# A seventh gather buffer, a sum-first joint between two token tiles, and four gate units moved into the second tile's block

## The chip, the core and the metric

The kernel runs on one core of a Trainium2 chip. The metric is the device time of one execution in microseconds, taken as the median of several runs. Five engines work beside each other: TensorE (PE; PEld is its weight loading), VectorE (DVE), ScalarE (ACT), GpSimd (POOL) and SyncE (SP). Each works its own queue in order and waits on semaphores. Sixteen DMA engines carry all transfers.

## The reference

One layer of each of two blocks is computed on 256 tokens of width 1024 in float32. The parts that matter here are these:

```
# first block, its last step: a product-key expert layer (PEER)
s = (h2 @ w_q) . sub_keys;  experts, g = top 16 of each of 8 heads      # 128 experts per token
x = x + g2 * sum_k( g_k * gelu(<h2, u[expert_k]>) * v[expert_k] )
x = rmsnorm(x, final_g)
# second block
u = rms_norm(x, norm_pre_mix);  proj = u @ w_in     # hq hf hi hg | nq nkv ngate | ga gb
h = x + rms_norm((sigmoid(ga) * (y_a @ w_branch_a) + sigmoid(gb) * (y_b @ w_branch_b)) @ w_out)
v = rms_norm(h, norm_pre_mlp)
h = h + rms_norm(square(relu(v @ w_up)) @ w_down, norm_post_mlp)        # width 4096
e = (p @ w_ple) * sigmoid(h @ w_ple_gate)
out = h + rms_norm(e, norm_ple)
```

`y_a` is a gated linear recurrence (HGRN2), `y_b` a sparse attention.

## The kernel before, in words

The tokens are two tiles of 128 (t = 0, 1). Each weight matrix is read in units of 1 MB (128 partitions x 2048). SP loads the units in the order in which PE uses them (`UNITS`) into a ring of four buffers (`RING`), and each buffer is reloaded when PE has passed it. The second block runs for tile 0 and then for tile 1, each time over all its weights: 87 units per tile, of which the MLP has 32 and the PLE gate 4.

The expert layer needs 128 experts per token. One gather (POOL, `indirect_dma_start`) brings one expert per token, key and value together, 1 MB. For tile 0 the gathers run in a ring of 10 buffers, before the second block starts. For tile 1 they run beside tile 0's second block in a ring of `N_BUF1` = 6 buffers. DVE works them off in 64 pairs: `second_dot` (L2010) multiplies the key with the token and sums, ACT makes a factor of it (Gelu and scale, `pair_factors`, L1502 and L1505), and `second_value` (L2021) adds factor times value to `summed` and so frees the buffer (`freed1`). `summed` lies in `junk[:, 1]`, and the dots write their product to `junk[:, 0]`.

The pairs are spread by hand. The code of tile 0's second block, on DVE and on ACT alike, counts 120 `beat`s, and pair g is worked at beat 120 g / 64 (`pairs_at`). The beats lie so: 0 and 1 ahead of tile 0's first norms, 2 to 19 in the hq/hf and hi/hg projections, 20 to 46 in the recurrence's levels, 47 to 58 in the compressed attention, 59 to 74 in the attention's eight items, 75 to 82 after them and ahead of the product with branch_b, 83 to 86 beside w_out2, 87 behind the norm ahead of the MLP, and 88 to 119 in the MLP, two for each of its 16 steps. A step k of the MLP is `up(k)` (L1029, one column unit) and `down(k-1)` (L1095, one row unit).

`first_norms(t)` adds the expert sum to the residual (`add_peer` L1833 and L1834 for tile 0, L2154 and L2155 for tile 1), normalises it with `final_g` (L1795) and makes the normalised input of the second block (`hat_of` L2083). ACT supplies the sums of squares and roots (`square`, L1309 and L1311). PE turns that input (`turn`, L1072, eight transposes), ACT and DVE copy it into `act_t` (L1530, L2067), and the first projection (hq, hf) can start. For tile 1 this stands behind tile 0's post-MLP norm and the turn of `h`, and beside the four units of tile 0's PLE gate (`tile_rows`, L1059). That stretch is called the joint below.

`token_unit` (L1039) multiplies one token tile with one column unit. `take_turned` copies transposed rows, `take_sums` (L1325) copies sums out of PSUM, `next_row` loads a gain row.

## Time and profile before

| | |
|---|---|
| median of 3 runs | 1575.87 us (1572.7 to 1577.41) |
| the profiled execution, its own time | 1566.96 us |
| its span, first to last instruction | 1565.2 us |
| PE, PEld, DVE, ACT, POOL busy | 80%, 56%, 57%, 31%, 18% |
| mean granted TensorE clock | 0.916 of full |
| DMA, mean rate | 327 GB/s over the span |

The busy shares are means over stages with different limits. A PE that waits for weights counts as idle, and matmuls at the lower clock count as longer busy. The 40 slices of the page are 39.1 us each.

### The profile page before, as it was taken

Reading aid. Unit: us, or ns where it says so; the run is one execution under the profiler, and the core shown is the slowest. Engines: PE = TensorE matmul, PEld = TensorE weight load, DVE = VectorE, ACT = ScalarE, POOL = GpSimd, SP = SyncE. Lnnn points to the kernel's source line nnn. Section 1 sums busy time; section 2 is a strip of 40 time slices with the busy share of each in tenths; the row PEclk is TensorE's granted clock in tenths of the full one; section 3 lists DMA queues with packets and bytes.
Section 4 is the critical chain, followed back from the end, with each engine's and each line's share of the span. In section 5 each row is a group of like instructions: output and inputs, shape, how many; then the busy total and the mean of one; then the engine's idle time right before and its main releaser. Section 6 shows DMA issues by size and latency. Waiting matters only on the chain. (4 is left out here: it accounts for less than half of the span.)

```text
span 1565.2 us, 17793 instructions
## 1 busy us (share of the span) xinstructions
PE 1251.6 (80%) x6212; PEld 871.7 (56%) x6212; DVE 898.7 (57%) x1790; ACT 481.5 (31%) x1177; POOL 284.4 (18%) x295
## 2 busy tenths in 40 slices
PE   6998899998778847756856656877689997988996
PEld 3887576653323317655733523654359994746772
DVE  1866367577799856679969876544432534511001
ACT  2103432333323325334434732211132233611112
POOL 0121013344434432223212231221100000000000
PEclk6999899999999988978878877999989999999998
DMA  9991049999999998999998999999958665366883
GB/s 349 374 340 64 28 159 426 427 426 427 426 427 427 427 397 338 426 404 372 398 422 369 371 362 386 405 425 425 410 210 302 214 213 217 108 210 247 294 310 122
DMA packets 71987, 512.00 MB, mean 327 GB/s; under 512 B 8144, under 2 KB 8288, under 8 KB 10976
## 3 DMA queue, kind: packets, MB, share of 16 engines
q0 software_dynamic: 40400, 290.46, 45.3%
q1 hardware_dynamic: 30496, 216.78, 36.7%
q10 hardware_dynamic: 1008, 3.67, 0.7%
q8 instruction: 50, 0.82, 0.2%
q14 instruction: 33, 0.27, 0.0%
HBM read 509.83 MB, written 1.05 MB: 326 GB/s over the span
## 5 line engine op out<-in xcount | busy, mean ns | idle before, releaser
L1004 PE MATMUL bank<-arena,diag 128*128 128x512 f32 x512 | 240.9, 620 | 51.1 <-ACT diag L1485 51.1
L1029 PEld LDWEIGHTS bank<-act_t,ring 128*128 128x128 f32 x2048 | 245.4, 200 | 45.5 <-issue 38.5
L1029 PE MATMUL bank<-act_t,ring 128*128 128x128 f32 x2048 | 249.4, 283 | 26.0 <-DMA ring<-in_weights 20.3
L2010 DVE SCALAR_TENSOR_TENSOR junk<-arena,bank 128x1024 f32<-128x1024 f32 x128 | 155.7, 1216 | 122.3 <-DMA arena<-in_experts,arena 122.0
L640 POOL DMA_INDIRECT arena<-in_experts,arena x128 | 129.9, 1015 | 431.2 <-DVE junk L2021 398.4
L1004 PEld LDWEIGHTS bank<-arena,diag 128*128 128x128 f32 x512 | 97.2, 197 | 187.0 <-issue 107.3
L2004 DVE SCALAR_TENSOR_TENSOR junk<-arena,bank 128x1024 f32<-128x1024 f32 x128 | 154.1, 1220 | 71.0 <-DMA arena<-in_experts,arena 67.4
L616 POOL DMA_INDIRECT arena<-in_experts,arena x128 | 127.7, 998 | 300.8 <-PE bank L1004 176.2
L2021 DVE SCALAR_TENSOR_TENSOR junk<-arena,junk 128x1024 f32<-128x1024 f32 x127 | 162.5, 1280 | 5.9 <-ACT arena L1505 5.8
L1039 PE MATMUL bank<-ring,act_t 128*128 128x256 f32 x576 | 131.1, 387 | 9.9 <-DMA ring<-in_weights 9.7
L1095 PE MATMUL bank<-ring,arena 128*128 128x512 f32 x256 | 116.0, 596 | 14.9 <-DMA ring<-in_weights 13.4
L1039 PEld LDWEIGHTS bank<-ring,act_t 128*128 128x128 f32 x576 | 110.4, 194 | 28.0 <-issue 6.4
L1325 ACT ACTIVATE arena<-bank 128x512 f32<-128x512 f32 x72 | 42.3, 597 | 257.7 <-PE bank L1039 57.2
L1779 DVE RECIPROCAL stat<-stat 128x1 f32<-128x1 f32 x18 | 2.9, 164 | 178.8 <-ACT stat L1311 178.8
L1502 ACT ACTIVATE arena<-arena 128x2 f32<-128x2 f32 x64 | 13.0, 203 | 268.0 <-DVE junk L2010 267.9
L1095 PEld LDWEIGHTS bank<-ring,arena 128*128 128x128 f32 x256 | 46.2, 190 | 64.1 <-issue 61.8
L1135 PE MATMUL bank<-arena 128*128 128x128 f32 x256 | 41.9, 330 | 37.3 <-DVE arena L2129 37.3
L1476 ACT ACTIVATE arena<-arena 128x2 f32<-128x2 f32 x64 | 13.0, 203 | 187.5 <-DVE junk L2004 187.4
L1756 DVE SCALAR_TENSOR_TENSOR arena<-arena 128x256 f32<-128x256 f32 x112 | 63.2, 565 | 4.0
L1059 PE MATMUL bank<-ring,act_t 128*128 128x512 f32 x128 | 62.5, 651 | 3.3 <-issue 2.5
L1059 PE MATMUL bank<-ring,arena 128*128 128x512 f32 x144 | 63.2, 595 | 2.3 <-ACT arena L1663 1.6
L1135 PEld LDWEIGHTS bank<-arena 128*128 128x128 f32 x256 | 39.0, 239 | 39.0 <-DVE arena L2129 38.8
(284 smaller groups left out, 1609.5 us busy)
## 6 DMA issues: line engine op xcount, KB each, us to landing
ring<-in_weights SPq DMA_DIRECT2D x203, 1024.0 KB, 6.7
arena<-in_ada_weights POOLq DMA_DIRECT2D x16, 1024.0 KB, 7.9
arena<-in_experts,arena POOLq DMA_INDIRECT x256, 14.5
row<-in_rows_in ACTq DMA_DIRECT2D x6, 512.0 KB, 3.8
arena<-in_rpb POOLq DMA_DIRECT2D x4, 512.0 KB, 14.3
res<-in_x SPq DMA_DIRECT2D x1, 1024.0 KB, 10.6
arena<-in_ctx_in SPq DMA_DIRECT2D x1, 1024.0 KB, 9.4
arena<-in_keys_in POOLq DMA_DIRECT2D x1, 1024.0 KB, 8.4
```

The costliest lines, as they stand in the source:

```text
L616: pool.indirect_dma_start(bufs[k % N_BUF], None, experts, bass.IndirectOffsetOnAxis(expert[:, 0, k:k + 1].bitcast(U32), 0), bounds_check=N ...
L640: pool.indirect_dma_start(bufs1[k % N_BUF1], None, experts, bass.IndirectOffsetOnAxis(expert[:, 1, k:k + 1].bitcast(U32), 0), bounds_check ...
L1004: last = mm(bank(j), diag[:, k % 4, :], bufs[k % N_BUF][:, D + half * 512:D + half * 512 + 512], start=(k == 0), stop=(k == SLOTS - 1))
L1029: last = mm(b[:, at + m * P:at + m * P + P], w[:, c, m * P:m * P + P], act_t[:, c, t * P:t * P + P], start=(c == 0), stop=(c == C - 1))
L1039: last = mm(b[:, at:at + 256], act_t[:, c, t * P:t * P + P], w[:, c, :], start=(c == 0), stop=(c == C - 1))
L1059: last = mm(bank(j + half), chunk(2 * k + r), w[:, r * D + half * 512:r * D + half * 512 + 512], start=(k == 0 and r == 0), stop=(k == n - ...
L1095: last = mm(bank(s0 + half), own.hid[:, k % 2, r * P:r * P + P], w[:, r * D + half * 512:r * D + half * 512 + 512], start=(k == 0 and r == ...
L1135: last = mm(b[:, m * P:m * P + P], lhs[:, h, :], rhs[:, h, :], start=True, stop=True)
L1756: last = v.scalar_tensor_tensor(dst, w[:, c, :], silu_c[:, c, z:z + 1], dst, ALU.mult, ALU.add)
L2004: v.scalar_tensor_tensor(junk[:, k % 2, :], bufs[k % N_BUF][:, 0:D], 1.0, x_nat_at(0), ALU.mult, ALU.mult, accum_out=dots[:, 0, k:k + 1]). ...
L2010: v.scalar_tensor_tensor(junk[:, 0, :], bufs1[k % N_BUF1][:, 0:D], 1.0, x_nat_at(1), ALU.mult, ALU.mult, accum_out=dots[:, 1, k:k + 1]).th ...
L2021: last = v.scalar_tensor_tensor(summed, value, by, summed, ALU.mult, ALU.add)
```

## The change

The ring for tile 1's gathers gets a seventh buffer, which is `junk`. The dot writes its product over the key that it has just used, and `summed` moves into the arena. The gain row for tile 1's first norm moves to gather buffer 3 of the ring, once that is free.

Pairs 0 and 1 (`EARLY`) are dotted inside tile 0's first norms, after the expert sum is added, and their values follow after the turn of `u`. The other 62 pairs are spread over 112 beats, so that the last falls on beat 110 and the last four steps of the MLP have none. In those steps `first_norms(1)` is done, so that `u` of tile 1 can be turned right behind tile 0's MLP.

Tile 0's PLE gate is cut into four column units (`late_gate`), worked in tile 1's block: after the first scores of the attention, between branch_b and the turn of `m`, between ple and the turn of `v`, and behind the MLP. The turn of tile 0's `h` stands behind tile 1's hq/hf projection. Tile 0's last norm and output come at tile 1's end. The small computation of the lower bounds (`lbt`) moves to the first block.

```diff
-N_BUF1 = 6
+N_BUF1 = 7
+LATE_GATE = {"gb": 0, "w_out2": 1, "mlp": 2, "ple_gate": 3}
-        bufs1 = [keys] + [bufs[n] for n in TURN]
+        bufs1 = [keys] + [bufs[n] for n in TURN] + [junk.rearrange("p t d -> p (t d)")]
-        summed = junk[:, 1, :]
-        row1 = arena[:, BUF_AT + 5 * UNIT - D:BUF_AT + 5 * UNIT]
+        summed = arena[:, BUF_AT + 5 * UNIT - D:BUF_AT + 5 * UNIT]
+        row1 = bufs1[ROW1_BUF][:, 0:D]
         N_BEATS = 120
+        LAST_BEAT = 112
+        EARLY = 2
-            return [g for g in range(PAIRS) if g * N_BEATS // PAIRS == beat]
+            return [g for g in range(EARLY, PAIRS) if g * LAST_BEAT // PAIRS == beat]
@@ POOL, tile 1's gathers
+                elif k < N_BUF1:
+                    pool.wait_ge(dots_ready, SLOTS)
@@ PE
+            def late_gate(k):
+                j = JOB["late_gate", k]
+                token_unit(UNITS["late_gate", k], open_job(j), 0, 0).then_inc(filled[bank_of[j]], 1)
...
                 for k in range(4):
                     unit_pair(column_unit, UNITS["hq_hf", t] + 2 * k, JOB["hqf", t] + k, t)
+                if t:
+                    pe.wait_ge(res_ready, RES_AT["mlp", 0])
+                    turn("h_t", 0, res[:, 0, :])
+                    all_emptied(JOB["h_t", 0], 2)
...
                 def gb_pair(r):
+                    if t and r == 0:
+                        late_gate(0)
...
                 tile_rows("branch_b", 4, t, lambda i: own.yb_t[:, i, :])
+                if t:
+                    late_gate(1)
                 pe.wait_ge(merged_ready, MERGED_AT["mix", t])
...
                 tile_rows("ple", 1, t, lambda i: pt[:, i, now])
+                if t:
+                    late_gate(2)
...
                 tile_mlp(t, own)
-                pe.wait_ge(res_ready, RES_AT["mlp", t])
-                turn("h_t", t, res[:, t, :])
-                all_emptied(JOB["h_t", t], 2)
-                tile_rows("ple_gate", 4, t, of_act)
+                if t:
+                    late_gate(3)
+                    pe.wait_ge(res_ready, RES_AT["mlp", t])
+                    turn("h_t", t, res[:, t, :])
+                    all_emptied(JOB["h_t", t], 2)
+                    tile_rows("ple_gate", 4, t, of_act)
@@ ACT
+            def take_late_gate(k):
+                j = JOB["late_gate", k]
+                is_filled(act, j)
+                fn(own_of[0].side[:, k * 256:k * 256 + 256], bank(j)[:, 0:256], ACT.Copy).then_inc(emptied[bank_of[j]], 1)
...
                 if t == 0:
-                    beat(t, 2)
-                    first_norms(0)
+                    load_root()
+                    first_norm(3, 0)
+                    first_norm(4, 0)
                     next_row(1)
+                    for g in range(EARLY):
+                        pair_factors(g)
...
                 for k in range(MLP_N):
...
                     beat(t, 2)
+                    if (t, k) == (0, MLP_N - 4):
+                        act.wait_ge(freed1[ROW1_BUF], len(range(ROW1_BUF, SLOTS, N_BUF1)))
+                        act.dma_start(row1, rows_in[0:1, :].broadcast_to([P, D])).then_inc(row1_loaded, 16)
+                    if (t, k) == (0, MLP_N - 3):
+                        first_norm(3, 1)
+                    if (t, k) == (0, MLP_N - 2):
+                        first_norm(4, 1)
-                load_root()
+                if t:
+                    load_root()
                 take_sums("mlp", t, own.side)
...
                 if t == 0:
                     take_turned("u_t", 1, "pre_mix")
                 square(7, t, own.side, own.gb)
+                if t:
+                    take_late_gate(3)
+                    take_turned("h_t", t)
+                    next_row(3)
...
+                    fn(last_gate, last_gate, ACT.Sigmoid).then_inc(gate_ready, 1)
+                    act.wait_ge(merged_ready, MERGED_AT["ple", 0])
+                    square(8, 0, first.ple, first.gb)
+                    take_sums("ple_gate", t, own.side, ACT.Sigmoid)
@@ DVE
             def second_dot(k):
-                v.scalar_tensor_tensor(junk[:, 0, :], bufs1[k % N_BUF1][:, 0:D], 1.0, x_nat_at(1), ALU.mult, ALU.mult,
+                key = bufs1[k % N_BUF1][:, 0:D]
+                v.scalar_tensor_tensor(key, key, 1.0, x_nat_at(1), ALU.mult, ALU.mult,
...
             def first_norms(t):
                 if t == 0:
...
                     add_peer()
+                    early_dots(0)
...
                 norm_gained(3, 0, t, res[:, t, :], res[:, t, :]).then_inc(res_ready, 1)
+                if t == 0:
+                    early_dots(1)
                 hat_of(4, t, own_of[t].hat3)
...
-                    beat(t, 2)
                     first_norms(0)
                     beat(t)
                     take_turned("u_t", t, "pre_mix")
...
+                    for k in range(GROUP * (EARLY - 1)):
+                        second_value(k)
...
                 beat(t, 2 * MLP_N)
-                add_normed(7, t, own.side, 2, own.hat)
-                take_turned("h_t", t)
                 if t == 0:
                     first_norms(1)
                     take_turned("u_t", 1, "pre_mix")
+                add_normed(7, t, own.side, 2, own.hat)
```

## Rows read from the trace of the kernel before

**Rows 1.** The page: one engine row, and the DMA row of the 40 slices.
```profile
PE 1251.6 (80%) x6212; PEld 871.7 (56%) x6212; DVE 898.7 (57%) x1790; ACT 481.5 (31%) x1177; POOL 284.4 (18%) x295
...
DMA  9991049999999998999998999999958665366883
```

**Rows 2.** The view by windows: stretch, each engine's busy time, granted clock, DMA share, GB/s.
```profile
573.00:597.00 24.00, 2.74 (x11) 2.37 (x12) 13.70 (x26) 8.34 (x20) 2.97 (x3) 0.54 0.75 282
596.00:676.00 80.00, 65.85 (x416) 59.02 (x416) 54.60 (x86) 31.93 (x53) 18.23 (x18) 0.96 0.99 408
676.00:776.00 100.00, 63.54 (x402) 61.36 (x401) 90.74 (x126) 41.42 (x69) 27.79 (x26) 0.80 0.98 385
776.00:840.00 64.00, 45.06 (x230) 28.91 (x230) 47.57 (x69) 26.69 (x53) 12.50 (x12) 0.81 0.94 389
840.00:920.00 80.00, 41.66 (x257) 32.92 (x256) 71.66 (x111) 50.23 (x134) 22.15 (x23) 0.77 0.94 369
920.00:976.00 56.00, 34.17 (x83) 15.29 (x81) 32.83 (x45) 12.12 (x35) 11.50 (x12) 0.83 0.97 396
...
1040.00:1060.00 20.00, 15.25 (x82) 10.22 (x82) 9.96 (x13) 2.74 (x10) 3.96 (x4) 1.00 1.01 425
```

**Rows 3.** The chain that ended last, at the joint: start, us, what.
```profile
1143.10 16.57 PE bank L1059 x32
...
1161.79 28.82 PE bank L1029 x256
```

**Rows 4.** The timeline at the joint: start, us, engine, line, [idle before <-releaser].
```profile
1124.33 3.70 PE L1095 MATMUL bank<-ring,arena 128*128 128x512 f32 x8 [1.51 <-ACT arena L1703]
...
1142.91 2.66 DVE L2021 SCALAR_TENSOR_TENSOR junk<-arena,junk 128x1024 f32<-128x1024 f32 x2
...
1153.09 0.75 DVE L2083 TENSOR_SCALAR arena<-res,stat 128x1024 f32<-128x1024 f32 x1
```

**Rows 5.** The timeline at the start of tile 0's second block.
```profile
573.91 1.22 DVE L2010 SCALAR_TENSOR_TENSOR junk<-arena,bank 128x1024 f32<-128x1024 f32 x1 [5.93 <-DMA arena<-in_experts,arena]
...
583.35 0.69 DVE L1833 TENSOR_TENSOR bank<-bank,arena 128x512 f32<-128x512 f32 x1
...
587.34 1.28 ACT L1311 ACT_TABLE_LOAD   x1
588.64 0.29 ACT L1311 ACTIVATE stat<-stat,eps 128x1 f32<-128x1 f32 x1
...
596.23 20.93 PE L1029 MATMUL bank<-act_t,ring 128*128 128x128 f32 x160 [1.27 <-ACT act_t L1530]
```

**Rows 6.** The waits in the MLP, 976 to 1128: DVE's own for gathers (us, times, longest).
```profile
DVE junk L2010 <- DMA arena<-in_experts,arena: 69.8, 27, 4.8
```

**Rows 7.** POOL's timeline: the first and the last of 30 gathers issued in the MLP.
```profile
979.14 0.99 POOL L640 DMA_INDIRECT arena<-in_experts,arena  x1 [17.91 <-DVE junk L2021]
...
1114.95 0.99 POOL L640 DMA_INDIRECT arena<-in_experts,arena  x1 [3.94 <-DVE junk L2021]
```

**Rows 8.** The chain that ended last, in tile 1's block.
```profile
1264.21 6.91 PE bank L1039 x32
...
1393.43 13.99 PE bank L1059 x32
...
1427.06 3.44 PE bank L1095 x8
1430.50 3.57 PE bank L1029 x32
```

**Rows 9.** PE's timeline at four places of tile 1's block.
```profile
1325.33 0.66 PE L783 MATMUL bank<-c,arena 128*128 128x128 f32 x4 [2.54 <-DVE arena L2303]
...
1391.51 1.09 PE L1072 MATMUL bank<-c,arena 128*128 128x128 f32 x8 [2.11 <-DVE arena L2324]
...
1414.92 1.97 PE L1072 MATMUL bank<-c,arena 128*128 128x128 f32 x8 [4.08 <-DVE arena L2083]
...
1537.04 1.66 PE L1072 MATMUL bank<-c,res 128*128 128x128 f32 x8 [5.02 <-DVE res L2080]
```

More of the change, by code:

```diff
@@ L75 @@
                           ("ple", 1), ("mlp", 32), ("ple_gate", 4)):
+        if _t == 0 and _name == "ple_gate":
+            continue
+        if _t == 1 and _name in LATE_GATE:
+            UNITS["late_gate", LATE_GATE[_name]] = _n
+            _n += 1
         UNITS[_name, _t] = _n
@@ L402, in build @@
         merged_ready = sem("merged_ready")
+        gate_ready = sem("gate_ready")
         stored = sem("stored")
@@ L1387, in na_sum @@
                     .then_inc(emptied[bank_of[s]], 1)
+            act.wait_ge(lb_ready, 1)
+            fn(lbt[:, 1:3, :], lbt[:, 1:3, :], ACT.Exp).then_inc(lb_ready, 1)
             for r in range(N_NA // 2 + 2):
@@ L1560, in second_block @@
                     beat(t, 2)
+                if t:
+                    take_turned("h_t", 0)
+                    next_row(1)
                 for k in range(4):
@@ L1672, in second_block @@
                             at_copy(n)
+                    if t and r == 0:
+                        take_late_gate(0)
                     if r in GB_AT[t]:
@@ L1708, in second_block @@
                     is_emptied(act, JOB["mlp", t] + half)
-                square(7, t, own.side, own.gb)
-                take_turned("h_t", t)
-                next_row(3)
-                if t == 0:
-                    first_norms(1)
-                take_sums("ple_gate", t, own.side, ACT.Sigmoid)
                 if t == 0:
                     take_turned("u_t", 1, "pre_mix")
-                load_root()
-                act.wait_ge(merged_ready, MERGED_AT["ple", t])
-                square(8, t, own.ple, own.gb)
-                if t == 0:
-                    act.wait_ge(res_ready, RES_AT["ple", 0])
-                    next_row(1)
+                square(7, t, own.side, own.gb)
+                if t:
+                    take_late_gate(3)
+                    take_turned("h_t", t)
+                    next_row(3)
+                    last_gate, first = own_of[0].side, own_of[0]
+                    for k in range(4):
+                        is_emptied(act, JOB["late_gate", k])
+                    fn(last_gate, last_gate, ACT.Sigmoid).then_inc(gate_ready, 1)
+                    act.wait_ge(merged_ready, MERGED_AT["ple", 0])
+                    square(8, 0, first.ple, first.gb)
+                    take_sums("ple_gate", t, own.side, ACT.Sigmoid)
+                    load_root()
+                    act.wait_ge(merged_ready, MERGED_AT["ple", t])
+                    square(8, t, own.ple, own.gb)
             for t in range(TT):
@@ L1888, in _ @@
                     na_normalise(k - 1)
+            dve.wait_ge(lb_ready, 2)
+            link(v.tensor_tensor(lbt[:, 3, :], lbt[:, 1, :], lbt[:, 2, :], ALU.add))
+            link(v.reciprocal(lbt[:, 0, :], lbt[:, 3, :]))
+            link(v.tensor_tensor(lbt[:, 4, :], lbt[:, 1, :], lbt[:, 0, :], ALU.mult))
+            link(v.tensor_scalar(lbt[:, 5, :], lbt[:, 4, :], -1.0, 1.0, ALU.mult, ALU.add))
             for k in range(2):
@@ L2017, in second_value @@
                 if k == 0:
+                    dve.wait_ge(freed[4], len(range(4, SLOTS, N_BUF)))
                     last = v.tensor_scalar(summed, value, by, None, ALU.mult)
@@ L2140, in level_take, with early_dots @@
                                       bank(j).rearrange("p (h t) -> p h t", h=4)).then_inc(emptied[bank_of[j]], 1)
+            def early_dots(g):
+                for k in range(g * GROUP, g * GROUP + GROUP):
+                    second_dot(k)
             def first_norms(t):
@@ L2336, in second_block @@
                     take_turned("u_t", 1, "pre_mix")
+                add_normed(7, t, own.side, 2, own.hat)
+                if t == 0:
+                    return
+                take_turned("h_t", t)
+                first = own_of[0]
+                for k in range(2):
+                    is_emptied(dve, JOB["ple", 0] + k)
+                dve.wait_ge(gate_ready, 1)
+                v.tensor_tensor(first.ple, first.ple, first.side, ALU.mult).then_inc(merged_ready, 1)
+                add_normed(8, 0, first.ple, 3, first.hat)
                 for k in range(2):
@@ L2404 @@
     stages.update({(name, t): units for name, units in block.items() for t in range(TT)})
+    stages.update({("late_gate", k): [unit] for k, unit in enumerate(column_units(a["w_ple_gate_2"][0]))})
     weights = _np.empty((N_UNITS, P, UNIT), _np.float32)
```

74 lines of the change are left out of this document (38 added, 36 removed).

## The prediction

> **What bounds the kernel now.** I read the page first. No engine is busy throughout, PE for 80% of the span and DVE for 57%, and the DMA row stands at 9 or 8 from slice 7 to slice 28 and drops behind them [rows 1]. That stretch is tile 0's second block with tile 1's gathers beside it, so the kernel has to be read by stages. The windows do that [rows 2]. In the MLP the DMA engines move 425 GB/s at a share of 1.01: that is the ceiling, and one unit or one gather (1.048 MB) costs 2.46 us there. Set against 425, the six stages ahead of the MLP leave DMA idle for 8.1, 3.2, 9.4, 5.4, 10.5 and 3.8 us (length times the missing part of the rate), 40 us in all. From 676 to 776 and from 840 to 920 DVE is busy for 91 and 72 us of 100 and 80: there DVE is the bound, with the pairs mixed into its own work.
>
> The waits say the same of the MLP: DVE's dots wait 69.8 us in 27 waits for gathers [rows 6], and a gather is issued every 4.92 us, because each waits for a value to free a buffer [rows 7]. A step of tile 0's MLP carries two units and two gathers, 9.85 us; a step of tile 1's MLP, without gathers, takes 3.44 + 3.57 = 7.0 us on PE [rows 8].
>
> Then the joint. PE's last matmuls of tile 0's MLP start at 1124.33 and run 3.70, so they end at 1128.03 [rows 4]. Tile 1's first projection starts at 1161.79, and 16.57 us of the 33.76 between are the PLE gate [rows 3]. It pays a cold clock: the same 32 matmuls take 13.99 us in w_out2 [rows 8]. The last two values run only at 1142.91, and the input of tile 1's turn is ready at 1153.09 + 0.75 [rows 4]: DVE works this off beside the gate, but in front of it PE stands still for the post-MLP norm. Behind the joint tile 1's block is bound by PE.
>
> **The joint.** With the sum and both norms done in the MLP's last steps, PE turns `u` right behind the last `down`. From the end of the gate (1143.10 + 16.57 = 1159.67) to 1161.79 the turn and its copies now take 2.1 us [rows 3]. I take 2.4, since ACT first copies the MLP sums. Term: 2.4 - 33.8 = -31.4. For this the norm must be ready. Now it takes 10.9 us from the first of the last two values to the end of L2083 [rows 4]. The last pair falls on beat 110, in step 11. When ACT gets back to work behind it, PE still has `down` 12 to 15 and `up` 14 and 15, 3.44 x 4 + 3.57 x 2 = 20.9 us. The chain has room, even if ACT takes it up one step later (7.0). If that cover were gone, each us of lateness costs one us. The post-MLP norm of tile 0 runs under tile 1's projection (28.82 us [rows 3]) and is hidden.
>
> **The gate units in tile 1's block.** Two token units take 6.91 us, so one takes 3.45 [rows 8]. The four places [rows 9]: (0) PE idles 2.54 us ahead of the first transposes, but the unit stands ahead of the second pair of scores, which feed DVE's next maximum, so I count 3.45 less a 2.3 us part of that wait: +1.1. (1) PE idles 2.11 ahead of the turn of `m`: 3.45 - 2.11 = +1.3. (2) PE idles 4.08: hidden; its PSUM bank shifts the MLP's banks to one that ACT frees at that time, +0.6. (3) PE idles 5.02: hidden. The turn of tile 0's `h` behind the hq/hf projection makes PE wait for one turn (1.09) and a copy of 0.7 to 0.8: +1.9. Queued behind it are the hi/hg units, with nothing late behind them, since DVE's recurrence work has those 27 us to catch up. Sum +4.9. Bounds: all five hidden but the turn, +1.9; none hidden, 4 x 3.45 + 1.9 + 0.6 = +16.3.
>
> The last norm of tile 0 (one gate Sigmoid over 1024, product, square, root, add, with three table loads) is put beside tile 1's PLE gate. A table load is 1.28 [rows 5], the pieces on ACT and DVE are near 1.2 each: some 9 us against at least 13.99 of PE work [rows 8]. Hidden; the output's transfer starts ahead of tile 1's. If it were not, the excess would be on the path.
>
> **The start of tile 0's block.** DVE works pairs 0 and 1 before it adds the expert sum: its first dot is at 573.91, `add_peer` at 583.35 [rows 5]. Now the sum comes first, at 573. The two early pairs' dots fall partly into DVE's waits for ACT's roots; the third and fourth gather set the pace there (2.46 each), and the table load at 587.34, on the path now, is moved ahead. I step through it: sum 573.0 to 575.8, two dots to 578.4, norm to 579.9, two dots to 582.4, `hat` to 583.4, turn and copies as now (2.4 plus 0.9), projection from 586.7 instead of 596.23. So 9.5 us earlier. One gather fewer has landed by then, as values 0 and 1 free their buffers later: net -7.0, which is 8.1 us of DMA idle [rows 2] less what remains. Bounds: -9.5 and 0, if the gathers that are then late take it back.
>
> At this place a page bears on the size. A table load costs 1.28 in this trace and the next ACT instruction follows within 0.02 us of its end. The Trainium skill (ScalarE: Activation LUTs, What ACT_TABLE_LOAD costs) adds a drain, for about 2.66 us per switch. By that, the load that leaves this path would give back 1.4 us more, a term of -8.4 where the row gives -7.0.
>
> **Pairs moved out of the MLP.** By 120 g / 64 the MLP has pairs 47 to 63, by 112 g / 64 it has 51 to 63. The four that leave it land: one in the projections, one in the compressed attention, one among the attention's eight items, one at beat 87. A pair costs DVE 2 x (1.22 + 1.28) = 5.0 (dots [rows 5], values [rows 4]), or DMA 2 x 2.46 = 4.9. In the projections and in the attention I count 4.9 and 5.0 in full; in the compressed attention 3.5, as DVE is busy for only 47.6 of 64 us there [rows 2]. The pair at beat 87 stands on DVE and on ACT ahead of the copies of the turned `v`: the MLP starts later by 3.5 (5.0 less the 1.5 us of turn and first copies that it runs beside). Sum +16.9. The seventh buffer lets one more gather be fetched while DVE is the bound and used when DMA is; that happens twice up to here, so -4.9 at most, and I take -3.5. The MLP then starts at 976.6 - 7.0 + 16.9 - 3.5 = 983.0.
>
> What the MLP gives back: 30 gathers are issued in it now [rows 7]. Then 26 belong to its pairs, of which all but about 21 are issued already (seven buffers, two of them still held by the pair before). With 26 units that PE and the ring take until the last gather lands, DMA has 47 transfers, 115.6 us: 1098.6. Then 24 us on PE for what is left (20.9 and 3 us for ACT to get from the last dot to the next hidden part). The MLP ends at 1122.6 instead of 1128.0: -5.4. Bounds: +4 (no gain from the buffer, the four pairs at 5.0 each: +6.6, and 3 less from the start) is a change of -5.4 + 6.6 + 3 = +4.2; the other way, with the four pairs taken up in DMA's idle time for half, -5.4 - 8.5 = -13.9.
>
> Small edits (`lbt` earlier, `summed` in the arena, the gain row on ACT's queue in step 12) cost nothing: they lie beside PE work or replace an equal instruction. The row's wait in step 12 is for value 122, two pairs before the last; if it were late, relu 13 and with it PE would be late. The dot in place is not in the trace; its nearest rows are the dot at 1.22 (another target) and the value at 1.28, which writes over its own input [rows 4, 5]. I take 1.22; at 1.28 it would cost 0.06 x 128 = 8 us of DVE, at most half of it on the path, +4.
>
> **Sum.** -31.4 + 4.9 - 5.4 = -31.9. The profiled execution took 1566.96, so 1535.1; its span 1533.3. The median of the runs shown is 8.9 us (0.57%) above the profiled execution, so the median comes to 1575.87 - 31.9 = 1544.0.
>
> **Rivals.** (a) *The pairs are not given back.* The stages ahead of the MLP are bound by DVE for 180 us, and each moved pair costs 5 there, while the last four steps of the MLP leave DMA idle: 28.0 us on PE against 8 units, 19.7 us of DMA. For it: the PE waits in the attention are already for DVE's work between pairs. Against it: 69.8 us of DVE's waits in the MLP are for gathers. The MLP ends at +4 to +10: total about -20, 1556. Chance 0.17.
>
> (b) *The gate units do not fit in the waits*, because each delays what DVE or ACT waits for next. The block grows by 16.3 and not 4.9: -20.5, 1555. Against it: three of four stand ahead of a wait that is for a norm or a gate that PE does not feed. Chance 0.10.
>
> (c) *DMA's idle time is used up.* The seventh buffer and the earlier start keep DMA busy, and the moved pairs cost half: -40, 1536. In the trace units and gathers share the MLP evenly, one of each per 4.92 us [rows 7]. With equal shares a further gather does not slow the weights that PE waits for, only the other gathers, so that the pair in the projections costs PE 0 and not 4.9; with half of the rest, that is where this time comes from. The Trainium skill states such a rule (DMA: Bandwidth & Descriptors, Queues, rings and completion order): each engine takes the queues in turn, packet by packet. The trace agrees as far as the 4.92 goes. Chance 0.16.
>
> (d) *Slower: the dot in place.* It reads and writes the same rows of a buffer that a transfer has just filled. If it took 0.5 us longer, DVE would have 64 us more in 128 dots, 50 of them in the 99 dots ahead of the MLP, nearly all on the path there: +50 - 31.9 = +18, 1594. It decides from 0.32 us per dot (31.9 / 99). Against it: the value in place costs 0.06 more than the dot [rows 4, 5]. Chance 0.03. (e) *It does not do what it says*: the norms of tile 1 are not ready when the MLP ends, since ACT takes them up behind relu 13 and 14, so PE waits some 8 to 12 us: -22, 1554. Chance 0.06.
>
> The forecast itself has 0.48.
>
> **Range and chances.** Its own range is 1537 to 1551, from the bounds of the MLP term (-13.9, +4.2) taken to half and those of the gate units. With (a), (b), (c) and (e) the range is 1532 to 1560. A difference under 0.3% (4.7 us) can't be told from no change here. All cases but (d) lie more than that below. Faster 0.94, same 0.02, slower 0.04, where the rest over (d) is left for a wait that I have not seen.
>
> **What would show it.** In the changed profile: tile 1's first projection follows the last `down` of tile 0's MLP within 3 us, with no stretch of low clock; `add_peer` starts near 573 and the projection near 587; the MLP of tile 0 starts near 983, its first steps go at about 9.9 to 10.5 us and its last three at 7.0; dots at 1.22; L1039 in four new places, with the waits of [rows 9] shrunk by its 3.45; `gate_ready` and the output of tile 0 well ahead of the end of the PLE gate. I am wrong if the attention stage (840 to 920) grows by over 10 us, if PE waits for tile 1's turn, or if the MLP's last steps stay near 9.9.

## The result, and the profile after

The changed kernel takes 1537.8 us in the median of 4 runs (1534.66 to 1538.34) against 1574.5 for the kernel before: a ratio of 0.9766 with a 95% interval of 0.9745 to 0.9787, 36.8 us less. A later set of its runs gave 0.9758 (0.9729 to 0.9787). The forecast was 1544.0 (1532 to 1560), so the time lies in its range and 6 us below its centre. The two profiled executions, 1566.96 and 1534.66, are 32.3 us apart, where the sum came to 31.9; against the changed kernel profiled again (1541.92) it is 25.0. Single executions scatter by more than the terms do, and the profiled one of before was faster than all of those timed for its median. The interval of the ratio is 33.5 to 40.1 us, so the 31.9 of the sum lies just below it: some 5 us of the gain stand in no term.

The DMA row of the changed kernel's page answers to [rows 1]. It drops at the same slice as before, to 7 where 5 stood; slices of 38.3 us are too coarse to show how the MLP ends.

```profile
DMA  9992039999999999999999989999978565368884
```

The windows of the changed kernel, cut at the same events as [rows 2] and with the MLP's last 31 us as a row of their own (length, PE, PEld, DVE, ACT, POOL, granted clock, DMA share, GB/s):

```profile
563.00:587.00 24.00, 9.90 (x26) 4.66 (x26) 14.04 (x27) 10.59 (x29) 3.94 (x4) 0.76 0.95 397
587.00:667.00 80.00, 65.53 (x416) 58.65 (x416) 48.60 (x67) 27.42 (x48) 22.34 (x19) 0.97 0.99 409
667.00:767.00 100.00, 55.31 (x363) 53.72 (x364) 95.71 (x138) 42.77 (x71) 31.14 (x28) 0.76 0.98 399
767.00:834.00 67.00, 46.27 (x251) 33.17 (x250) 52.50 (x70) 30.24 (x59) 15.62 (x16) 0.80 0.97 403
834.00:919.00 85.00, 45.24 (x241) 33.84 (x240) 75.84 (x120) 50.24 (x132) 22.99 (x23) 0.75 0.93 373
919.00:983.00 64.00, 40.47 (x117) 19.62 (x115) 44.46 (x60) 16.54 (x46) 15.82 (x16) 0.82 1.00 411
983.00:1095.00 112.00, 88.59 (x480) 62.90 (x481) 60.56 (x78) 17.14 (x60) 21.21 (x21) 0.98 1.01 424
1095.00:1126.00 31.00, 31.00 (x166) 21.39 (x165) 8.56 (x9) 8.64 (x20) 0.00 (x0) 1.00 0.85 314
```

Against 425 GB/s DMA stands idle for 26.7 us in the six stages ahead of the MLP, where it was 40.4. 8.1 of that come back as idle time at the MLP's end, where PE is busy for 31.0 of 31 us.

The timeline at the start of tile 0's block, against [rows 5], and at the joint, against [rows 3, 4]:

```profile
572.48 0.70 DVE L1895 TENSOR_TENSOR bank<-bank,arena 128x512 f32<-128x512 f32 x1 [4.08 <-PE bank L1026]
...
583.58 1.97 PE L1094 MATMUL bank<-c,arena 128*128 128x128 f32 x8 [10.39 <-DVE arena L2157]
...
586.82 5.46 PE L1051 MATMUL bank<-act_t,ring 128*128 128x128 f32 x24 [1.27 <-ACT act_t L1570]
...
1093.75 1.22 DVE L2083 SCALAR_TENSOR_TENSOR arena<-arena,bank 128x1024 f32<-128x1024 f32 x1 [2.53 <-DMA arena<-in_experts,arena]
...
1114.33 0.75 DVE L2157 TENSOR_SCALAR arena<-res,stat 128x1024 f32<-128x1024 f32 x1
...
1118.71 7.03 PE L1117 MATMUL bank<-ring,arena 128*128 128x512 f32 x16
...
1127.88 7.38 PE L1051 MATMUL bank<-act_t,ring 128*128 128x128 f32 x64 [1.27 <-ACT act_t L1570]
```

The sum is added at 572.48 and the projection starts at 586.82. Tile 1's normalised input is ready at 1115.08, ten microseconds before the MLP ends at 1125.74, and the projection follows 2.1 us behind that end.

PE's chain in tile 1's block, against [rows 8, 9]; the unit of L1061 with x16 is a gate unit:

```profile
1293.26 3.65 PE bank L1061 x16
...
1360.92 3.45 PE bank L1061 x16
...
1509.54 13.99 PE bank L1081 x32
```

Cut at these events, the executions compare so (us; the first column from the end of the first tile's last expert matmul; each a difference of two starts or ends in PE's timeline):

| kernel | to the projection | to MLP start | MLP | joint | tile 1's block |
|---|---|---|---|---|---|
| before | 23.5 | 380.4 | 151.4 | 33.8 | 403.4 |
| changed | 13.6 | 396.1 | 142.9 | 2.1 | 405.0 |
| changed, profiled again | 13.7 | 400.1 | 142.4 | 2.1 | 406.7 |

The executions of equal code show what a stage can tell. gates_behind_mlp and thin_gates, below, differ from the changed kernel only behind tile 0's MLP, so their first columns are two more executions of it: 400.0 and 399.8 to the MLP's start, 141.7 and 141.4 in the MLP. So 396.1 is the lowest of four, and the others lie within 0.3 us of 400. before_112 has the tile 1 block of the kernel before, in 409.1 us where that took 403.4. The changed block was profiled in nine executions, with 403.5 to 407.0 us and a mean of 405.8. What stands ahead of the first column ends anywhere from 567.4 to 579.2 us, so absolute times tell little, and the stages are counted from there.

### The profile page after: what moved, and what is told of

Same layout as the page of the kernel before. It is cut to its first block, busy times and chain, and to the rows that moved or that the text cites. A ratio compares the mean times of both kernels' runs of the same rounds, so it can differ in the third digit from the quotient of the medians.

```text
span 1532.9 us, 17865 instructions
## 1 busy us (share of the span) xinstructions
PE 1245.2 (81%) x6244; PEld 874.6 (57%) x6244; DVE 897.8 (59%) x1790; ACT 484.2 (32%) x1180; POOL 290.0 (19%) x295
## 4 chain that ended last, share of the span: by engine, by line
PE 43%; DMA 24%; DVE 17%; issue 10%; ACT 4%; POOL 1%; SPq 0%; DVEq 0%; ACTq 0%; POOLq 0%
DMA arena<-in_experts,arena 12%; PE bank L1051 9%; DMA ring<-in_weights 8%; PE bank L1026 5%; PE bank L1117 5%; PE bank L1081 5%; PE bank L1061 5%; DVE arena L1818 3%; PE bank L948 3%; DMA arena<-in_ada_weights 2%; PE bank L917 2%; DVE arena L2083 2%; PE bank L1165 1%; DMA junk<-in_experts,arena 1%; DVE arena L2095 1%
## 5 line engine op out<-in xcount | busy, mean ns | idle before, releaser
L1051 PE MATMUL bank<-act_t,ring 128*128 128x128 f32 x2048 | 246.2, 281 | 26.5 <-DMA ring<-in_weights 17.0
L2076 DVE SCALAR_TENSOR_TENSOR junk<-arena,bank 128x1024 f32<-128x1024 f32 x128 | 154.1, 1220 | 71.2 <-DMA arena<-in_experts,arena 67.8
L636 POOL DMA_INDIRECT arena<-in_experts,arena x128 | 127.0, 992 | 302.7 <-PE bank L1026 177.3
L2083 DVE SCALAR_TENSOR_TENSOR arena<-arena,bank 128x1024 f32<-128x1024 f32 x110 | 134.0, 1218 | 81.5 <-DMA arena<-in_experts,arena 81.2
L662 POOL DMA_INDIRECT arena<-in_experts,arena x110 | 116.7, 1061 | 328.4 <-DVE arena L2095 293.3
L1061 PE MATMUL bank<-ring,act_t 128*128 128x256 f32 x640 | 147.3, 389 | 11.4 <-DMA ring<-in_weights 9.7
L1061 PEld LDWEIGHTS bank<-ring,act_t 128*128 128x128 f32 x640 | 123.7, 196 | 33.3 <-issue 8.2
L2095 DVE SCALAR_TENSOR_TENSOR arena<-arena 128x1024 f32<-128x1024 f32 x109 | 139.8, 1282 | 4.2 <-ACT arena L1545 3.9
L1542 ACT ACTIVATE arena<-arena 128x2 f32<-128x2 f32 x64 | 12.9, 202 | 202.7 <-DVE arena L2083 176.8
L1752 ACT ACTIVATE arena<-bank 128x256 f32<-128x256 f32 x32 | 12.3, 383 | 162.2 <-PE bank L1051 162.2
```

The lines of the kernel that those rows point to most:

```text
L636: pool.indirect_dma_start(bufs[k % N_BUF], None, experts, bass.IndirectOffsetOnAxis(expert[:, 0, k:k + 1].bitcast(U32), 0), bounds_check=N ...
L662: pool.indirect_dma_start(bufs1[k % N_BUF1], None, experts, bass.IndirectOffsetOnAxis(expert[:, 1, k:k + 1].bitcast(U32), 0), bounds_check ...
L1051: last = mm(b[:, at + m * P:at + m * P + P], w[:, c, m * P:m * P + P], act_t[:, c, t * P:t * P + P], start=(c == 0), stop=(c == C - 1))
L1061: last = mm(b[:, at:at + 256], act_t[:, c, t * P:t * P + P], w[:, c, :], start=(c == 0), stop=(c == C - 1))
L2076: v.scalar_tensor_tensor(junk[:, k % 2, :], bufs[k % N_BUF][:, 0:D], 1.0, x_nat_at(0), ALU.mult, ALU.mult, accum_out=dots[:, 0, k:k + 1]). ...
L2083: v.scalar_tensor_tensor(key, key, 1.0, x_nat_at(1), ALU.mult, ALU.mult, accum_out=dots[:, 1, k:k + 1]).then_inc(dots_ready, 1)
```

## The experiments

Each was timed over several rounds beside the kernel before. Ratios are to that kernel, and the changed kernel stands at 0.9766 and 0.9758. The table has the stages of each profiled execution, in the columns of the one above.

| kernel | ratio (95%) | to MLP start | MLP | joint | tile 1's block |
|---|---|---|---|---|---|
| six_buffers | 0.9839 (0.9798 to 0.9881) | 409.3 | 143.4 | 2.1 | 406.6 |
| gates_behind_mlp | 0.9803 (0.9771 to 0.9835) | 400.0 | 141.7 | 2.1 | 415.9 |
| thin_gates | 0.9799 (0.9762 to 0.9836) | 399.8 | 141.4 | 2.1 | 407.7 |
| pairs_first | 0.9781 (0.9745 to 0.9817) | 393.8 | 142.5 | 2.2 | 406.8 |
| last_beat_104 | 0.9878 (0.9853 to 0.9903) | 429.5 | 132.0 | 2.1 | 404.8 |
| last_beat_116 | 0.9744 (0.9716 to 0.9771) | 388.8 | 154.3 | 2.1 | 406.5 |
| last_beat_118 | 0.9801 (0.9776 to 0.9827) | 389.8 | 150.0 | 8.5 | 407.0 |
| copies_first | 0.9751 (0.9724 to 0.9779) | 395.5 | 144.7 | 2.1 | 405.1 |
| before_112 | 1.0036 (1.0019 to 1.0054) | 400.0 | 143.7 | 25.8 | 409.1 |
| copies_first_114 | 0.9739 (0.9710 to 0.9767) | 388.4 | 147.9 | 2.1 | 403.5 |

**The seventh buffer: six_buffers.**

```diff
-N_BUF1 = 7
+N_BUF1 = 6
-        bufs1 = [keys] + [bufs[n] for n in TURN] + [junk.rearrange("p t d -> p (t d)")]
+        bufs1 = [keys] + [bufs[n] for n in TURN]
```

> The changed kernel with six gather buffers for tile 1 instead of seven, all else as changed. My count for the seventh buffer is 3.5 us: two stretches bound by DVE, each hands one fetched gather (2.46 us) to a stretch bound by DMA. So 3.5 us slower than the changed kernel (2.5 to 4.9), seen as a later end of tile 0's MLP (1129 instead of 1125.6), with more DMA idle between 590 and 983. Rival: the buffer gives nothing, since where DVE is the bound a freed buffer is refilled in time with six as well: within 1 us.

It costs 0.0073 to 0.0081 of 1574.5, about 12 us, over three times my count; the intervals leave some 2 to 21. The stage ahead of the MLP shows it too: 409.3 against the four of 396.1 to 400.1. The windows of both kernels over nearly that stage (the one with six first):

```profile
582.00:989.00 407.00, 256.35 (x1379) 201.69 (x1378) 315.48 (x448) 166.40 (x354) 104.32 (x99) 0.80 0.96 386
```

```profile
588.00:981.00 393.00, 251.69 (x1379) 197.83 (x1377) 314.23 (x446) 165.71 (x352) 106.92 (x99) 0.82 0.98 400
```

DVE has the same work, 315.5 and 314.2 us, but DMA moves 386 GB/s instead of 400. DVE's waits for gathers in this stage (us, times, longest), with six buffers and then with seven, where the new buffer `junk` has a line of its own:

```profile
DVE arena L2083 <- DMA arena<-in_experts,arena: 55.5, 28, 3.0
```

```profile
DVE arena L2083 <- DMA arena<-in_experts,arena: 40.1, 21, 2.5
DVE junk L2083 <- DMA junk<-in_experts,arena: 4.7, 2, 2.5
```

DVE waits 55.5 us for gathers with six buffers and 44.8 with seven (44.2 in the other execution): 11 us, which is the size of the loss. The buffer is not used twice, as I had counted: 28 waits have become 23. My explanation is that the hand-spread beats come in lumps (own work, then a pair), and that with one gather more under way fewer lumps leave DMA without a free buffer; the lumps themselves were not varied.

**The start of tile 0's block: pairs_first.**

```diff
 # DVE
-                    add_peer()
-                    early_dots(0)
+                    add_peer()
...
-                    first_norms(0)
+                    for g in range(EARLY):
+                        pair_share(g)
+                    first_norms(0)
...
 # ACT
-                    load_root()
+                    for g in range(EARLY):
+                        pair_factors(g)
                     first_norm(3, 0)
                     first_norm(4, 0)
                     next_row(1)
-                    for g in range(EARLY):
-                        pair_factors(g)
```

> The changed kernel with pairs 0 and 1 worked ahead of the expert sum in tile 0's first norms, as before the change, and without the early table load. The first projection starts 9.4 us later (596 instead of 586.8). By my forecast 2.5 us of it come back through one gather more that has landed by then: 7 us slower at the end of tile 0's MLP and in the total. Rival: the stretch behind it is bound by DMA, which is idle for some microseconds less only, so that less than 3 us are left at the end.

PE's timeline of it:

```profile
599.46 1.97 PE L1094 MATMUL bank<-c,arena 128*128 128x128 f32 x8 [20.24 <-DVE arena L2156]
```

PE waits 20.24 us there instead of 10.39. From the last expert matmul (575.52 + 3.70) to the projection (602.70) it is 23.5 us again, as before the change. From that matmul to the end of tile 0's MLP it is 559.8 us against 552.5 in the changed kernel: 7.3 later, as forecast; but the three other executions of that code have 556.1, 555.3 and 554.8, so it is 3.7 to 7.3. The ratio puts it at 0.9781, 2 to 4 us above the changed kernel, with an interval that covers both 0 and 7. The 9.9 us at the projection are shown. That some are left at the end rests on one execution against four, and how many is not settled.

**Where the MLP's time comes from: last_beat_104, last_beat_116, last_beat_118, before_112.**

```diff
-        LAST_BEAT = 112
+        LAST_BEAT = 104      # last_beat_104
...
+        LAST_BEAT = 116      # last_beat_116; the row in step 13, the norms in 14 and 15
...
+        LAST_BEAT = 118      # last_beat_118; the row in step 14, the norms in 15 and behind the MLP
...
-            return [g for g in range(PAIRS) if g * N_BEATS // PAIRS == beat]
+            return [g for g in range(PAIRS) if g * 112 // PAIRS == beat]      # before_112
```

> The changed kernel with the pairs spread over 104 beats instead of 112: 9 pairs are left in the MLP instead of 13. Four more pairs ahead of it cost 16.9 us by the forecast's prices. Theory A, the forecast's (the MLP lasts as long as the transfers up to the last gather, each 2.46 us, and then PE): 12 transfers fewer and two PE steps more give back 29.5 - 14 = 15.5, so +1.4 us. Theory B (weights and gathers share DMA evenly while both have work, so a step takes 9.85 us while gathers last and 7.0 behind them, and each gather moved out turns half a step from 9.85 to 7.0): it gives back 4 x 2.85 = 11.4, so +5.5 us.

PE's timeline of last_beat_104, where its last gathers land:

```profile
1074.21 3.81 PE L1051 MATMUL bank<-act_t,ring 128*128 128x128 f32 x32 [1.29 <-DMA ring<-in_weights]
1079.14 3.67 PE L1117 MATMUL bank<-ring,arena 128*128 128x512 f32 x8 [1.12 <-DMA ring<-in_weights]
1084.07 3.81 PE L1051 MATMUL bank<-act_t,ring 128*128 128x128 f32 x32 [1.25 <-DMA ring<-in_weights]
1087.71 3.60 PE L1117 MATMUL bank<-ring,arena 128*128 128x512 f32 x8
1091.15 3.73 PE L1051 MATMUL bank<-act_t,ring 128*128 128x128 f32 x32
```

and of the changed kernel:

```profile
1084.16 3.81 PE L1051 MATMUL bank<-act_t,ring 128*128 128x128 f32 x32 [1.30 <-DMA ring<-in_weights]
1089.09 3.67 PE L1117 MATMUL bank<-ring,arena 128*128 128x512 f32 x8 [1.12 <-DMA ring<-in_weights]
1094.05 3.81 PE L1051 MATMUL bank<-act_t,ring 128*128 128x128 f32 x32 [1.28 <-DMA ring<-in_weights]
1097.69 3.60 PE L1117 MATMUL bank<-ring,arena 128*128 128x512 f32 x8
```

Units start 4.93 us apart while gathers run, each behind a wait for its own load, and 3.5 apart at once when they end (last dots at 1087.27 and 1093.75). The MLP of last_beat_104 is 9.4 to 10.9 us shorter than the four, nearer theory B's 11.4 than A's 15.5. Ahead of the MLP its four pairs cost 29 to 33 us, not 16.9, and the ratio says +18 us, where the theories had +5.5 and +1.4.

> The changed kernel with the pairs spread over 116 beats, and the gain row, the first and the second norm of tile 1 each one MLP step later: 15 pairs in the MLP instead of 13. Two pairs fewer ahead of it save 8.4 us. Theory A gives 7.7 of them back (six transfers at 2.46 less one PE step): -0.7 us. Theory B gives 2 x 2.85 = 5.7 back: -2.7 us. In both the norms of tile 1 are still ready when the MLP ends.

The ratio gives 2 to 4 us less than the changed kernel, with overlapping intervals. The stage ahead is 7.2 to 11.3 us shorter. The MLP is 11.4 to 12.9 longer, where A gave 7.7 and B 5.7. 2.6 of it is a wait that neither had, in this timeline:

```profile
1117.72 1.06 ACT L1347 ACTIVATE arena<-res 128x1024 f32<-128x1024 f32 x1 [5.21 <-DVE res L2234]
...
1121.25 5.26 PE L1117 MATMUL bank<-ring,arena 128*128 128x512 f32 x8 [2.56 <-ACT arena L1754]
```

The first norm is queued on ACT ahead of the last hidden part; it waits 5.21 us for DVE's expert sum, and PE waits 2.56 for the hidden part and then runs the `down` at a lower clock (5.26 us instead of 3.60, another 1.7). That leaves 7 to 9 us for two pairs, which is A's number and not B's. So B, which is nearer in last_beat_104, is not confirmed here.

> The changed kernel with the pairs spread over 118 beats, the gain row in step 14, the first norm in step 15 and the second behind the MLP: 16 pairs in the MLP. Theory B alone: three pairs fewer ahead save 12.6, three steps at 9.85 cost 8.5, -4 us. Rival: the norms come too late by then, as ACT takes up the second one only behind the last hidden part, and PE waits 3 to 6 us ahead of tile 1's turn: 0 to +2 us.

Its timeline:

```profile
1131.61 1.97 PE L1094 MATMUL bank<-c,arena 128*128 128x128 f32 x8 [5.26 <-DVE arena L2159]
```

The norms come too late: PE idles 5.26 us and turns at the lower clock, the joint is 8.5 instead of 2.1, and the ratio is 0.9801, 5 to 7 us above the changed kernel, more than the 0 to 2 of the rival. The joint grows by the rival's reason. With the last pair in step 13 (last_beat_116) it was still 2.1 us, with the last pair in step 14 and the second norm behind the MLP it is 8.5; so the last pair has to lie some two MLP steps ahead of the end.

> The kernel before, with its pairs spread over 112 beats instead of 120 and nothing else: six buffers, gate in the joint, norms of tile 1 behind the MLP. My forecast priced the four pairs that leave the MLP at 16.9 us ahead of it; with what theory B gives back in the MLP (11.4 us) the kernel would get 5.5 us slower. The run with six buffers suggests more: there the stretch from the first projection to the MLP was 29 us longer than before the change, and the MLP 8 us shorter. If that is the spread's price without the seventh buffer, this kernel is 15 to 20 us slower than before.

The ratio says 5.7 us slower (3.0 to 8.5), the first of the two numbers, but by other parts. The stage ahead of the MLP is 19.6 us longer, the MLP 7.7 shorter, and the joint 7.9 shorter, since the last values no longer come after the MLP. PE's timeline there:

```profile
1141.04 1.97 PE L1072 MATMUL bank<-c,res 128*128 128x128 f32 x8 [5.02 <-DVE res L2080]
```

5.02 us of idle time ahead of this turn, where PE stood for 12.3 from 1128.03 to 1140.30. 7.3 us of the 33.8 in the joint were thus the last pair's lateness, which the profile of before showed as a norm's. Its rows, read again, have the chain:

```profile
1131.44 1.22 DVE L2010 SCALAR_TENSOR_TENSOR junk<-arena,bank 128x1024 f32<-128x1024 f32 x1 [2.50 <-DMA arena<-in_experts,arena]
...
1132.71 0.20 ACT L1502 ACTIVATE arena<-arena 128x2 f32<-128x2 f32 x1 [8.43 <-DVE junk L2010]
...
1133.44 1.28 ACT L1321 ACT_TABLE_LOAD   x1
...
1140.30 1.97 PE L1072 MATMUL bank<-c,res 128*128 128x128 f32 x8 [12.27 <-DVE res L2080]
```

PE has ended the MLP at 1128.03, but ACT stands in front of the last pair's factors until the last gather has landed and its dot is done, and only behind them loads the table for the norm. In before_112 that load is done 4.7 us before the MLP ends (1131.32 against 1136.02).

These three make +3.9. The MLP's own 7.7 lies below B's 11.4, so B gives back too much as well. The profiled execution also starts its projection 3.9 us earlier than that of before and takes 5.6 longer in tile 1's block, and the spread touches neither: that is the scatter of single executions. In the block it comes with a lower clock in equal code (branch_a's 32 matmuls 16.50 us instead of 13.98, w_out2's 15.67 instead of 13.97).

**The gate units: gates_behind_mlp and thin_gates.**

```diff
 # gates_behind_mlp: none in the attention, behind branch_b and behind ple
-                    late_gate(3)
+                    for k in range(4):
+                        late_gate(k)
...
 # thin_gates
-                token_unit(UNITS["late_gate", k], open_job(j), 0, 0).then_inc(filled[bank_of[j]], 1)
+                u, b = UNITS["late_gate", k], open_job(j)
+                w = unit(u).rearrange("p (c n) -> p c n", c=C)
+                last = mm(b[:, 0:256], act_t[:, 0, 0:P], w[:, 0, :], start=True, stop=True)
+                pass_previous(last, u)
+                last = mm(b[:, 0:64], act_t[:, 1, 0:P], w[:, 1, 0:64], start=True, stop=True)
+                last.then_inc(filled[bank_of[j]], 1)
```

> The changed kernel with all four gate units behind tile 1's MLP, none in the three earlier waits. If the waits alone count: the wait behind the MLP covers 5.0 us of 13.8, so 8.8 us lie open there, and the 1.1 and 1.1 us that the first two cost go away: 6.5 us slower. If the units also keep the clock at 2.4 GHz in what follows them, the three places lose that too (1.0 after the first scores, 0.9 in the turn of v, 1.5 at the start of the MLP): 10 us slower.

> The changed kernel with each late gate unit cut from eight accumulating matmuls to one and a quarter; tile 0's PLE gate is then not computed in full. All units are still loaded and passed. If only the fit into the waits counts, the places in the attention and ahead of the turn of m give back 1.1 and 1.1 us: 2 us faster. If the units keep the clock up, the stretches behind them fall back to the times of before (the first scores 1.0, turn of v 0.9, start of the MLP 1.5, turn of h 0.6, last gate 2.3 us, 6 in all): 3 to 4 us slower than the changed kernel, although PE does 11 us less work.

The windows over the first scores, the turn of `v`, the MLP's start and the last gate: the changed kernel, gates_behind_mlp (the turn of `v`, the MLP's start and the scores; its last gate, right behind the four units, takes 13.97 us) and thin_gates.

```profile
1291.00:1306.00 15.00, 11.67 (x83) 8.82 (x81) 11.36 (x33) 7.89 (x28) 0.00 (x0) 1.00 0.32 117
1379.00:1392.00 13.00, 10.78 (x51) 7.39 (x49) 4.71 (x9) 6.47 (x15) 0.00 (x0) 1.00 0.80 280
1392.00:1402.00 10.00, 10.00 (x69) 8.09 (x68) 0.00 (x0) 1.60 (x4) 0.00 (x0) 1.00 0.74 275
1507.00:1524.00 17.00, 15.07 (x40) 6.86 (x40) 5.15 (x6) 7.99 (x10) 0.00 (x0) 1.00 0.37 129
```

```profile
1379.00:1392.00 13.00, 7.65 (x27) 4.15 (x26) 4.71 (x9) 6.20 (x14) 0.00 (x0) 0.89 0.57 202
1392.00:1402.00 10.00, 10.00 (x64) 9.17 (x63) 0.00 (x0) 1.60 (x4) 0.00 (x0) 0.80 0.62 211
1291.00:1306.00 15.00, 10.84 (x67) 7.77 (x66) 11.50 (x33) 7.04 (x24) 0.00 (x0) 0.77 0.15 62
```

```profile
1291.00:1306.00 15.00, 10.40 (x76) 7.70 (x75) 11.70 (x34) 8.90 (x30) 0.00 (x0) 1.00 0.38 133
1378.00:1390.00 12.00, 7.25 (x28) 4.95 (x27) 4.71 (x9) 5.71 (x14) 0.00 (x0) 0.82 0.73 273
1390.00:1402.00 12.00, 12.00 (x76) 10.09 (x76) 0.00 (x0) 1.60 (x4) 0.00 (x0) 0.90 0.70 234
1507.00:1524.00 17.00, 15.52 (x35) 7.18 (x36) 5.18 (x6) 6.95 (x8) 0.00 (x0) 0.80 0.35 130
```

The granted clock is full in the changed kernel and 0.77 to 0.90 where the units are missing or thin; only the first scores of thin_gates stay at full clock, as some work is left there. Tile 1's block of gates_behind_mlp is 8.9 to 12.4 us longer than those of the nine executions with the units in the waits (10.9 and 9.2 against the two of the changed kernel), where the waits alone gave 6.5 and the clock 10. thin_gates does some 11.6 us less work on PE (6.75 of 8 matmuls in four units of 3.45), and its block of 407.7 us is 1.9 us longer than the mean of the nine and longer than each, not 2 shorter. Up to the end of tile 1's MLP it is level (374.5 against 374.7), and from there to the end 33.2 against 30.3: the last gate runs at 0.80 of the clock. The clock theory holds in the rows, with 10 us forecast for the first and 3 to 4 for the second. The timed runs do not settle it. By the ratios gates_behind_mlp is 6 to 7 us slower than the changed kernel, which is what the waits alone gave, and thin_gates 5 to 7, where the waits alone gave 2 faster; both intervals overlap those of the changed kernel.

**A better version: copies_first, copies_first_114, and the changed kernel again.**

```diff
 # DVE and ACT, tile 0 and tile 1 alike
-                beat(t)
-                take_turned("v_t", t, "pre_mlp")
+                take_turned("v_t", t, "pre_mlp")
+                beat(t)                           # on ACT behind take_sums("ple", ...)
 # copies_first_114, besides
-        LAST_BEAT = 112
+        LAST_BEAT = 114
```

> The changed kernel with the copies of the turned v ahead of the pair at beat 87, on DVE and on ACT. The MLP starts 4 to 5 us earlier (978 to 979 instead of 982.9). If the MLP's end is set by how many steps run at 9.85 us, the gain stays at the end but for what the later pair costs: 2 to 4 us faster. If it is set by the number of transfers up to the last gather, the end stays: within 1 us.

The MLP starts 3.2 us behind the turn of `v`, no longer 6.5, and lasts 144.7 us instead of 141.4 to 142.9. 1.8 to 3.3 of the 3.3 us won are lost again, so the two readings are not told apart; the ratio, 1.1 to 2.4 us below the changed kernel's, is within the noise.

> The changed kernel with the copies of the turned v ahead of the pair at beat 87, and the pairs spread over 114 beats: one pair more in the MLP, the norms of tile 1 in the same steps as changed. By theory B the pair saves 4.2 to 8 us ahead of the MLP and costs 2.9 in it, while the last pair now falls on step 12, one step ahead of the first norm: 1 to 5 us faster than the changed kernel. Rival: the first norm then waits in step 13 for the expert sum, ACT holds up the hidden part behind it, and PE waits 2 to 3 us: no gain.

> The changed kernel itself once more, beside these two on the same chip, so that they can be compared with it as well as with the kernel before. 0.9766 of the time before, within 0.003.

copies_first_114 has the lowest ratio of all, 0.9739, and 1533.5 us against 1537.5 for the changed kernel on the same chip. From the projection to the end of the MLP it takes 536.3 us against 538.9 to 542.5 in the four. PE has no wait for ACT in its last steps, so the rival did not come. The intervals of the two ratios overlap, so the gain of 3 to 4 us is likely and not shown.

## Why the prediction was right, step by step

The forecast of 1544.0 is 6 us above the time, and part of that nearness is luck: the term of the MLP's end promised some 5 us too much, the gate units were priced 3 to 5 us too high, and the two errors cancel. What carries the prediction is the joint, and its mechanism is shown.

**The joint.** 31.4 us was forecast and 33.8 - 2.1 = 31.6 came. The norms are ready 10 us ahead of need. What I had not seen is that 7.3 us of the joint were the wait for the last pair; before_112 shows that the new spread alone takes them away, so they are not won by the norms' new place.

**The start of tile 0's block.** 9.5 us forecast at the projection, 9.9 measured. Of the 7.0 that should remain, pairs_first shows 3.7 to 7.3. The drain that the Trainium skill adds to a table load (ScalarE: Activation LUTs, What ACT_TABLE_LOAD costs) is not seen: the load at 1118.89 in last_beat_116 takes 1.28 us, and the next ACT instruction starts at 1120.18.

**The MLP's start.** 983.0 was forecast and 982.9 came, and that it fits to a tenth is luck. Counted from the last expert matmul the start was to move by +6.4 us; it moved by +5.8 in that execution and by 9.6 to 9.9 in the three others. Two terms of the sum were mis-sized against each other. The seventh buffer was counted at 3.5 us and is worth about 12. The four pairs were counted at 16.9, and cost 19.6 without the buffer in before_112 (one execution against one); four further pairs cost 29 to 33 in last_beat_104. There DVE has 20 us more to do than in the changed kernel (335.9 us busy against 317), and PE takes 10 us more for the same matmuls (261.8 against 252) at a clock of 0.78 instead of 0.82; in the window of the levels the clock is 0.80 before the change, 0.76 behind it and 0.72 in last_beat_104. So the price rises with the number of pairs, and the falling clock fits it; that it is the cause was not tested. How the buffer and the number of pairs share the sum was not taken apart further.

**The MLP's end.** Forecast -5.4. From the last expert matmul it was 555.3 us before, and is 552.5, 556.1, 555.3 and 554.8 in the four executions: -2.7 to +0.9, -0.6 in the mean. So the stage gained next to nothing, and the term was mis-sized. Half of the difference is the late start above. The other half is the MLP itself, for which the sum has 139.6 us and which takes 141.4 to 142.9. The step that failed there is "DMA has 47 transfers, 115.6 us: 1098.6. Then 24 us on PE". The last gather's dot came at 1093.75, and PE still had 32 us to go. Weights do not run ahead of the gathers; both go at one per 4.93 us, so PE is later in its steps when the last gather lands than a count of all transfers says. The rule on turns between queues in the Trainium skill (DMA: Bandwidth & Descriptors, Queues, rings and completion order) fits these rows. I had used it for rival (c) and not in the sum. Rival (c) itself, that moved pairs cost half (8.5 us for four), is refuted by last_beat_104 and before_112, where four cost 29 to 33 and 19.6.

**The gate units.** Forecast +4.9. The first pair of executions has +1.6, but equal code differs by more: nine executions of the changed block have 405.8 us in the mean, and the old block took 403.4 in before and 409.1 in before_112. So the units cost nothing that can be told from zero. Place by place, the first pair of executions shows why. The turn of `h` costs 1.8 (forecast 1.9), the first gate unit delays the transposes by 1.2 (1.1), the second the turn of `m` by 1.1 (1.3). The failed step is what follows: the text priced the four waits as time and not as a stretch in which the clock falls. With PE busy in them, the first scores take 1.1 us less, the turn of `v` 0.9, the MLP's start 1.5, the last gate 2.3 (13.99 instead of 16.32), and the turn of `h` behind the MLP 0.6. The MLP's start and the last gate, before and changed:

```profile
1418.15 8.91 PE L1029 MATMUL bank<-act_t,ring 128*128 128x128 f32 x64 [1.26 <-ACT act_t L1530]
...
1539.53 16.30 PE L1059 MATMUL bank<-ring,act_t 128*128 128x512 f32 x32 [0.83 <-issue]
```

```profile
1390.25 7.38 PE L1051 MATMUL bank<-act_t,ring 128*128 128x128 f32 x64 [1.59 <-ACT arena L1363]
```

These two hold over all executions: the last gate takes 13.97 us in all nine and 16.30 and 16.75 in before and before_112, the MLP's start 7.38 in eight of nine (9.01 in last_beat_104) and 8.91 and 10.01. Some 3.4 us are lost between the short units of the compressed attention and the scores, where the window at branch_a shows 0.92 and 1.00 before the change. That need not be the change: branch_a's 32 matmuls take 13.98 to 16.72 us in the nine, and 13.98 and 16.50 in before and before_112.

**The small edits.** The dot in place takes 1.218 us (1.215 before), so rival (d) falls. The last norm of tile 0 is done at 1518.2, under the last gate, which ends at 1523.5. Rivals (a) and (b) did not come; (a) was right in that moved pairs are not given back, but the buffer paid for them. Rival (d) counts 99 dots ahead of the MLP; with pairs 0 to 50 there they are 102, which changes nothing.

## What to carry to other kernels

Where two streams share a saturated DMA, count the consumer's steps that run at the shared rate (here 4.93 us per unit instead of 3.5) and not the bytes: a transfer moved out of such a stretch gives back less than it costs elsewhere, unless something waits for the last one. Independent matmuls put into PE's waits were worth more here than the waits they filled, as what followed ran at the full clock; so price a wait with the low-clock stretch behind it. One buffer more in a ring whose consumer works in lumps was worth about 12 us, several times the 2.46 of one transfer. And a term of 5 us can't be read from one execution against one where equal code scatters by 4 to 6.

## What the runs showed that was not expected

The same kernel's stage from the first projection to the MLP takes 396.1 us in one execution and 400.1 in another, with the granted clock at 0.82 and 0.81 and PE busy for 252 and 256 us with the same matmuls; so a difference below 4 us there says nothing. The 64 matmuls at the MLP's start of tile 1 take 7.38 us at the full clock and 8.91 where the window over them shows 0.81 (the kernel before, 1418 to 1427). The wait of ACT for a norm, 5.21 us in last_beat_116, costs PE 2.56 us of standing and 1.66 more in the next eight matmuls, which take 5.26 us instead of 3.60.
